# Operand tiles of the split matmuls moved by 32 bytes in their buffers

## What is computed

```python
h = modulate(rms_norm(x, norm1_g), sh1, sc1)
z = h @ w_in                                   # 1024 x 11520
y_att, y_conv, y_rwkv = attention(z), conv(z), rwkv7(z)
x = x + (1 + gt1) * ((g_att*y_att + g_conv*y_conv + g_rwkv*y_rwkv) @ w_out)
h = modulate(rms_norm(x, norm2_g), sh2, sc2)
q = (h @ w_q)                                  # queries of 8 heads
eid, gate = product_key_top16(q, key1, key2)   # 16 of 16384 experts per head
act = gelu(h . u[eid])                         # expert scores
x = x + (1 + gt2) * sum(gate * act * v[eid])   # expert mixing
```

## The kernel before

| tile | role | start mod 128 |
|---|---|---|
| `zw_hi`, `zw_lo`, `gw_hi`, `ow_hi`, `wq_hi`, `u_hi`, `u_lo` | weights of projections, queries, scores | 0 |
| `v_hi`, `v_lo` | streamed in mixing | 0 |
| `zh_hi` (217280) | streamed in projections, mostly | 64 |
| `zh_lo` (32896) | streamed in projections, mostly | 0 |
| `h_hi` (106688), `h_lo` (114880) | streamed in queries and scores | 64 |
| `w_hi` (219328), `w_lo` (221376) | weights of mixing | 64 |
| `m_hi`, `m_lo` | streamed in two output blocks | 64 |

## Time and profile before

### The profile page before, as it was taken

How to read it: one execution, slowest core, us unless ns; L and a number is a source line. 1 busy time by engine, 2 the same in 40 slices (tenths; PEclk the granted TensorE clock), 3 DMA queues, 4 the chain that set the end, 5 groups by cost and what they waited for, 6 DMA issues and landing times.

```text
span 2810.4 us, 51269 instructions
## 1 busy us (share of the span) xinstructions
PE 2724.6 (97%) x19786; PEld 2472.4 (88%) x19786; DVE 2239.4 (80%) x4318; ACT 1162.8 (41%) x1664; POOL 567.1 (20%) x354
## 2 busy tenths in 40 slices
PE   6999998999999999999999999999999999999998
PEld 6998887889999997787799988788999999987776
DVE  7998686579977658888879987756899766688887
ACT  4543422244554443333355343222455444433334
POOL 0000002110877730000000000030227686100000
PEclk9999999999999999999999999999999999999999
DMA  7553360466788778788745534434578887888885
GB/s 299 181 189 124 134 220 11 158 240 212 219 247 248 197 233 303 279 281 282 246 151 190 184 106 187 135 116 151 187 227 240 242 232 204 271 280 281 291 284 189
DMA packets 258985, 593.81 MB, mean 211 GB/s; under 512 B 82608, under 2 KB 198064, under 8 KB 200240
## 3 DMA queue, kind: packets, MB, share of 16 engines
q1 hardware_dynamic: 192656, 572.74, 58.4%
q0 software_dynamic: 36864, 0.15, 2.7%
q10 hardware_dynamic: 29216, 17.57, 2.1%
HBM read 537.27 MB, written 53.08 MB: 210 GB/s over the span
## 4 chain that ended last, share of the span: by engine, by line
PE 83%; DVE 11%; ACT 2%; issue 1%; DMA 1%; POOL 0%; DVEq 0%; SPq 0%; POOLq 0%; ACTq 0%
PE ps L1197 26%; PE ps L1176 20%; PE ps L687 13%; PE ps L649 6%; PE ps L777 2%; PE ps L1186 2%; DVE u_lo L2113 2%; PE ps L727 1%; PE ps L1062 1%; DMA ring<-in_stream 1%; PE ps L939 1%; DVE region L1721 1%; PE ps L1009 1%; DVE region L2164 1%; PE ps L996 1%
## 5 line engine op out<-in xcount | busy, mean ns | idle before, releaser
L1176 PE MATMUL ps<-h_hi,u_hi 128*128 128x256 f32 x2048 | 580.5, 283 | 3.3 <-DVE u_lo L2113 3.0
L1176 PE MATMUL ps<-h_lo,u_hi 128*128 128x256 f32 x2048 | 571.5, 279 | 0.0
L1176 PE MATMUL ps<-h_hi,u_lo 128*128 128x256 f32 x2048 | 570.9, 279 | 0.0
L2360 POOL DMA_INDIRECT gate_rows<-route x256 | 475.2, 1856 | 291.9 <-DVE route L2227 124.7
L2113 DVE TENSOR_TENSOR u_lo<-ring,u_hi 128x1024 fp32r<-128x1024 f32 x256 | 312.3, 1220 | 180.9 <-ACT u_hi L1513 169.1
L1176 PEld LDWEIGHTS ps<-h_hi,u_hi 128*128 128x128 f32 x2048 | 384.8, 188 | 7.1 <-DVE u_lo L2113 6.5
L1176 PEld LDWEIGHTS ps<-h_hi,u_lo 128*128 128x128 f32 x2048 | 384.2, 188 | 0.0
L1176 PEld LDWEIGHTS ps<-h_lo,u_hi 128*128 128x128 f32 x2048 | 384.0, 188 | 0.0
L1534 ACT ACTIVATE u_hi<-ring 128x1024 fp32r<-128x1024 f32 x192 | 203.9, 1062 | 323.7 <-PE ps L1197 323.7
L2120 DVE TENSOR_TENSOR u_lo<-ring,u_hi 128x1024 fp32r<-128x1024 f32 x192 | 234.7, 1223 | 50.9 <-ACT u_hi L1534 50.7
L1513 ACT ACTIVATE u_hi<-ring 128x1024 fp32r<-128x1024 f32 x256 | 269.3, 1052 | 0.0
(11 more groups left out here) (394 smaller groups left out, 5189.7 us busy)
## 6 DMA issues: line engine op xcount, KB each, us to landing
ring<-in_stream SPq DMA_DIRECT2D x456, 1024.0 KB, 7.6
act_rows<-region SPq DMA_DIRECT2D x256, 128.0 KB
gate_rows<-rstd ACTq DMA_DIRECT2D x2, 8192.0 KB, 29.6
region<-gate_rows SPq DMA_DIRECT2D x256, 64.0 KB, 3.9
region<-act_rows SPq DMA_DIRECT2D x128, 128.0 KB, 4.3
small_inverse<-act_rows SPq DMA_DIRECT2D x128, 128.0 KB, 4.2
gate_rows<-route POOLq DMA_INDIRECT x256
region<-in_c SPq DMA_DIRECT2D x7, 512.0 KB, 5.7
```

Of the source, the lines that this page charges most:

```text
L1176: ins = mm(ps[:, c % 4, 0:T], x, y[:, k, :], start=k == 0 and i == 0, stop=k == KD - 1 and i == 2)
L2360: gp.indirect_dma_start(gate_cells, bass.IndirectOffsetOnAxis(ap=gate_at[:, r:r + 1].bitcast(I32), axis=0), gate_weight[:, r:r + 1], None, ...
```

## The change

Four places are moved by 8 numbers, 32 bytes: `zh_hi` and `w_hi`, `w_lo` up, `h_hi` and `h_lo` down. Modulo 128 bytes `zh_hi` then starts at 96 and not at 64, `w_hi` and `w_lo` at 96, `h_hi` and `h_lo` at 32. All others stay: the weights of projections and scores and the streamed tiles of mixing at 0, `zh_lo` at 0, `m_hi` and `m_lo` at 64. The new places touch no other tile that is in use at that time: `zh_hi` reaches 32 bytes into `small_inverse`, which is not yet written then. No instruction is added, removed or moved on any engine, and every operand has the size that it had.

```diff
-        zh_hi, zh_lo = over(hot_at, "zh_hi", 0, KD, T), peer("zh_lo", 4096, KD, T)
+        zh_hi, zh_lo = over(hot_at, "zh_hi", 8, KD, T), peer("zh_lo", 4096, KD, T)
...
-        h_hi, h_lo = peer("h_hi", 22544, KD, T), peer("h_lo", 24592, KD, T)
+        h_hi, h_lo = peer("h_hi", 22536, KD, T), peer("h_lo", 24584, KD, T)
...
-        w_hi, w_lo = over(hot_at, "w_hi", 512, 2, T), over(hot_at, "w_lo", 1024, 2, T)
+        w_hi, w_lo = over(hot_at, "w_hi", 520, 2, T), over(hot_at, "w_lo", 1032, 2, T)
```

## The result

The changed kernel takes 2819.27 us, the median of 15 runs (2815.75 to 2832.26), beside 2814.57 for the kernel before (15 runs, 2811.57 to 2820.48). The ratio is 1.0017 [1.0009, 1.0025]: a loss of 4.7 us, clear of the noise, though within the 0.2% that the prediction counts as no change. The forecast was a gain of 28 us. The profiled execution of the changed kernel has a span of 2816.9 us, 6.5 more than before.

What follows compares the result with a forecast made beforehand. PE's own pace was taken as the bound; gains of 16.0 + 4 (scores), 6 (projections) and 2 (queries), 28.0 us off the profiled 2812.2, left 2784.2, and 4.0 up to the runs' median gave 2788.2 us; range 2754 to 2840.

Steps and rivals of the forecast that it cites:

- The second pair of rows: `split_block` matmuls before the change: 118.1 ns each with `zh_hi` streaming at 64, 119.4 with `zh_lo` at 0.
- I take the good state for the streams of 256 columns: Scores, queries and `zh_hi` were to reach 113.4 ns per matmul, from 117.6 to 118.1.
- The terms of 16.0 and 4 us for scores: Gains in scores: 16.0 us from chunk 40 of each layer on, 4 us in the 40 chunks before.
- that of 2 us for the queries: Gain in the queries: 3.2 us offered by the spacing, 2 taken because DVE is nearly full there.
- that of 6 us for the projections: Gain in the projections from moving `zh_hi`: 8.4 us by the spacing, 6 taken because of DVE.
- 0.36 + 0.12: Chances of the forecast (scores, queries, `zh_hi` reach the good spacing), 0.36, and of the same with mixing, 0.12.
- mixing at nothing: Mixing was left at 233 ns, no gain; bounds were 20.0 us won or 11.1 us lost.
- the far end: Mixing's furthest gain: 216 ns, as the plain float32 matmuls at L649 show, worth 52 us.
- the 24 us of cover: Between POOL's last indirect DMA (1024.15) and mixing's start (1048.92), said to take a gain of some 8 us per layer.
- The one of no effect (2816): Rival over all moved operands: 32 bytes don't matter or both lockings stay, time as before, 2816; chance 0.18.
- The slower rival: Rows starting mid-64 bytes touch one unit more; scores, queries, `zh_hi` at 119.4 ns, 24.8 us lost, 2841; chance 0.29.
- scores stay at 215: Sign in scores' windows: 215 matmuls in 25 us means the forecast is wrong; 223 was forecast.

Runs made afterwards that it cites:

- both_shifted: Against the kernel before, `u_hi`, `u_lo`, `h_hi`, `h_lo` moved together by 32 bytes, scores' distance still 64, `w_hi`, `w_lo` to 96; 2822.07 us in one run.
- quarter_three: Against the kernel before, `h_hi`, `h_lo` and mixing's stream put at distance 96, `zh_hi` at 32; 2825.99 us in one run.
- timed_112: Against the kernel before, distance 112 in scores, mixing and for `zh_hi`; 2796.99 us, median of 6 runs, ratio 0.9928.
- all_zero: Against the kernel before, `h_hi`, `h_lo`, `zh_hi`, `w_hi`, `w_lo` all start at 0 modulo 128 bytes, as their partners do; 2826.36 us, ratio 1.0037.
- still_flow: Places of the kernel before, but each score matmul streams its first column 256 times (results not the reference's); 2801.17 us.

## Why the prediction was wrong

**Right: PE's pace is the time.** With equal instructions in equal order, places alone moved the time from 2787 to 2826 us, and the spacing with it, while DVE's busy time moved by 3 us and ACT's by 2 in all kernels here (POOL's, of which the profile's spans are rough, by 20).

**Right: the place of operands relative to each other counts.** Moving both together (both_shifted) leaves scores their two spacings, moving one doesn't, in each stage apart. That nothing but this distance modulo 128 counts is not so: with all streams at 0, scores have 119.9 ns and projections 118.4. The second pair of rows from which I read it, 118.1 and 119.4 ns in the earlier trace rows, was thin too: over the matmuls of L687 in before, those that stream `zh_lo` at 0 (896) have 118.1 ns and those that stream `zh_hi` at 64 (1788) 118.0. The two ports of the Trainium skill ("SBUF — State Buffer", Who interferes with whom) would give zero; the measured places differ by 6 ns in scores, and the measurement decides. The Trainium skill ("SBUF — State Buffer", Operand start alignment) says of its rule only that it is about legality, so the zero that I drew from it was my own; here 48 bytes (64 to 112, in all three stages) are worth 18.4 us.

**Wrong, and decisive: "I take the good state for the streams of 256 columns".** From two points (0 and 64) I took it that a quarter of a period would hold the good spacing of the earlier trace rows. It doesn't hold the good one: 32 is worth 116.9 to 117.4 in scores, and 96, as far from 0 on the other side, is worse than 64: 119.5 in the projections (120.0 in scores, by quarter_three). The terms of 16.0 and 4 us for scores came out at 0, that of 2 us for the queries at 0 (117.8 and 117.7 ns), that of 6 us for the projections at -4.5. The good spacing does exist, at 112, a distance that no row of before showed. The two untried places were guesses by the prediction's own words, and I gave them 0.36 + 0.12, while scores hold the good spacing nearly throughout at one place in eight. The picture behind the choice, a stream and a load that meet in the memory, stays unproven.

**Wrong: mixing at nothing.** It lost 2.9 us by its spacing (0.95 ns; my bound for a loss was 3.6 ns each), and it does have faster places, among them one with two held spacings, 226.7 and 233.3. 226.7 is close to the bound that I worked out as twice 113.4; 216, the far end, was never seen.

**Wrong: the 24 us of cover.** I read the margin at POOL's last issue and at mixing's start. The wait that bites is SP's for the same DMAs, since stores for ACT are queued behind it, and it has no margin: ACT stands there in before already (11.7 us over both layers). The closing words on "a margin that I don't see" were the right worry at the wrong place. It cost the change nothing, and one execution of timed_112 some 7 us in layer one.

**The rivals.** The one of no effect (2816) came nearest to the time, but not by its reason: projections and mixing got slower, and the mean of scores stayed only because a gain in many of its chunks and a loss in the 24 fast ones cancel, which is luck. The slower rival had the direction, but its mechanism, a 64-byte unit more per row, fell with both_shifted and all_zero: in the latter every row starts at a multiple of 64 bytes, and scores go at 119.9. Its price of 24.8 us was far too high, as it put all stages at 119.4. The range (2754 to 2840) held the time; the sign that the prediction named for being wrong, "scores stay at 215", is what came (217, 216 and 215).

## What to carry to other kernels

Where PE is the bound, the distance between the streamed and the loaded tile may be worth trying: in this kernel it was worth 0.4% of loss to 0.7% of gain, free of any instruction, and stages had maps of their own. It couldn't be guessed from one or two points: measure the spacing at all eight multiples of 16, for several stages in one run, since here moving one stage's tiles left the others' spacing as it was. And look at which engine stands at a wait with other work queued behind it; here that was SP.

## What the runs showed of the hardware

- The start-to-start spacing of fp32r matmuls of 256 columns depends on the operands' distance: 113.3 to 120 ns by chunk, all at a granted clock of 1.00 (the 2.4 GHz level). With a stream that stands still it is 111.67 ns (still_flow). For 512 columns it is 226.7 to 234.3. The distance modulo 128 isn't all: at 0 scores have 119.9 and projections 118.4.
- Some distances have two spacings that are held for dozens of matmuls and change at an interruption (64 in scores, 113.3 and 117.8; 112 in mixing, 226.7 and 233.3), others just one (0 in scores).
- The Trainium skill ("TensorE: Matmul & The Clock Gate", Wait — 56ns, not 53.3ns?) would have 215.7 ns for 512 columns and 109.2 for 256, as its rule gives them. No fp32r matmul of this kernel came to that at any of eight distances.
- Left open: why the stream's walk loses time beside a load that stands still, what ties the best place to 112, whether the period is 128 bytes, and the projections with `zh_lo` moved too, which was not tried.
